# Hybrid decoder step, the last two output tiles split into 384 tokens and 136 in place of 260 and 260

## The reference, cut to what matters

```python
mix = concat([pm * silu(gp), a * silu(ga)], axis=-1)        # (tokens, 2048)
x = x + einsum('btm,md->btd', mix, w_out)                   # w_out: 2048 x 2048
y = x * rsqrt(mean(x * x, axis=-1) + 1e-6) * final_norm_g   # over all 2048 of a token
```

## Time and profile before

| | |
|---|---|
| median of 3 runs | 871.41 us (871.34 to 871.78) |
| the profiled execution | 871.79 us |
| its span | 869.8 us |
| TensorE matmul busy | 847.5 us, 97% of the span |
| VectorE, ScalarE, GpSimd busy | 545.9, 396.7, 40.1 us |
| granted TensorE clock, mean | 0.991 of full speed |

### The profile page before, as it was taken

One profiled execution on the slowest core, in us unless ns is written; L12 is line 12 of the kernel. 1 busy time (PEld: TensorE's weight loads), 2 busy tenths in 40 slices (PEclk: granted clock), 3 DMA queues, 4 the chain that ended last, 5 costly groups with the idle time before them and its releaser, 6 DMA issues.

```text
span 869.8 us, 17334 instructions
## 1 busy us (share of the span) xinstructions
PE 847.5 (97%) x6974; PEld 840.3 (97%) x6974; DVE 545.9 (63%) x1107; ACT 396.7 (46%) x917; POOL 40.1 (5%) x72
## 2 busy tenths in 40 slices
PE   7999999999999999999999999999999999999993
PEld 7999999999999999999999999999999999999993
DVE  5645875696668568747966785778877343333333
ACT  5745436523543454355345424543563444434332
POOL 2000000000000000000000001000000000000001
PEclk9999999999999999999999999999999999999997
DMA  9574266337525643563385247526658434334425
GB/s 289 149 178 129 83 157 158 102 107 175 143 82 137 186 120 95 151 168 108 89 187 141 86 135 196 136 75 150 172 161 281 139 95 129 113 115 120 135 62 196
DMA packets 207303, 122.45 MB, mean 141 GB/s; under 512 B 6552, under 2 KB 200608, under 8 KB 207200
## 3 DMA queue, kind: packets, MB, share of 16 engines
q1 hardware_dynamic: 204152, 113.86, 48.2%
q0 software_dynamic: 3072, 7.49, 2.5%
HBM read 106.59 MB, written 15.20 MB: 140 GB/s over the span
## 4 chain that ended last, share of the span: by engine, by line
PE 95%; DVE 2%; issue 1%; ACT 1%; DMA 1%; SPq 0%; DVEq 0%; ACTq 0%
PE pj L582 79%; PE ps_t L611 3%; PE pj L605 3%; PE ps_m L611 2%; PE ps_o L654 1%; PE ps_s L626 1%; PE ps_s L624 1%; PE ps_o L652 1%; PE ps_s L671 1%; PE ps_s L582 1%; PE ps_t L671 1%; PE ps_o L582 1%; DMA arena<-in_x_prompt 1%; PE pj L546 1%; DVE arena L1302 0%
## 5 line engine op out<-in xcount | busy, mean ns | idle before, releaser
L582 PE MATMUL pj<-mov_hi,w_hi 128*128 128x260 f32 x1952 | 403.8, 288 | 0.0
L582 PE MATMUL pj<-mov_hi,w_lo 128*128 128x260 f32 x1952 | 393.2, 283 | 0.0
L582 PE MATMUL pj<-mov_lo,w_hi 128*128 128x260 f32 x1952 | 392.5, 283 | 0.0
L582 PEld LDWEIGHTS pj<-mov_hi,w_hi 128*128 128x128 f32 x1952 | 300.9, 189 | 0.9
L582 PEld LDWEIGHTS pj<-mov_lo,w_hi 128*128 128x128 f32 x1952 | 301.3, 189 | 0.0
L582 PEld LDWEIGHTS pj<-mov_hi,w_lo 128*128 128x128 f32 x1952 | 301.0, 189 | 0.0
L1196 DVE TENSOR_TENSOR w_lo<-w_raw,w_hi 128x768 fp32r<-128x768 f32 (+1 forms) x189 | 163.5, 865 | 162.4 <-ACT w_hi L801 160.9
L801 ACT ACTIVATE w_hi<-w_raw 128x768 fp32r<-128x768 f32 (+1 forms) x189 | 145.7, 771 | 213.0 <-PE pj L582 195.6
L857 ACT ACTIVATE pt_hi<-ps_t 128x128 fp32r<-128x128 f32 (+1 forms) x64 | 26.2, 436 | 79.6 <-PE ps_t L611 75.4
L1279 DVE TENSOR_TENSOR pt_lo<-ps_t,pt_hi 128x128 fp32r<-128x128 f32 (+1 forms) x64 | 29.6, 483 | 43.2 <-ACT pt_hi L857 43.2
L1228 DVE SCALAR_TENSOR_TENSOR arena<-pj,rstd_bc 128x260 f32<-128x260 f32 (+2 forms) x104 | 36.9, 398 | 19.4 <-PE pj L582 17.8
(11 more groups left out here) (213 smaller groups left out, 806.3 us busy)
## 6 DMA issues: line engine op xcount, KB each, us to landing
w_raw<-in_w_in SPq DMA_DIRECT2D x96, 320.0 KB, 3.6
w_raw<-in_w_in SPq DMA_DIRECT2D x48, 384.0 KB, 3.8
arena<-in_cache_k_win SPq DMA_DIRECT2D x16, 384.0 KB
arena<-in_cache_v_win SPq DMA_DIRECT2D x16, 384.0 KB
w_raw<-in_w_out SPq DMA_DIRECT2D x16, 384.0 KB, 3.4
w_raw<-in_w_out SPq DMA_DIRECT2D x16, 320.0 KB, 3.1
arena<-in_cache_k_win SPq DMA_DIRECT2D x8, 512.0 KB
arena<-in_cache_v_win SPq DMA_DIRECT2D x8, 512.0 KB
```

The lines of the kernel that those rows point to most:

```text
L582: mm = pe.matmul(dst[h][:, 0:HT], w, m[:, k, HT * h:HT * h + HT], start=(k == 0 and i == 0), stop=(c == 2 and k == KT - 1 and i == 2))
```

## The change

The boundary between the two parts moves from token column 260 to 384 (HALF). Part 0 has 384 columns, row groups 0, 1 and 2; part 1 has 136, row group 3 and the samples. All that was laid out by halves follows: the transposes, evictions, adds and GpSimd's multiplications are 3 row groups wide in part 0 and 1 in part 1. ScalarE squares row groups 0 and 2 in part 0 and only the samples in part 1, VectorE squares row group 1 and then 3. In part 0 VectorE scales both halves of row group 0 and the first of 2, ScalarE both of 1 and the second of 2; in part 1 VectorE scales the first half of row group 3 (and the samples), ScalarE the second. Six stores of 512 KB follow part 0, two and the samples' follow part 1. The number of matmuls, their weights and the order on TensorE are the same.

```diff
+HALF = (0, 3 * P, NT)
@@ SP
-            for h in range(2):
-                for i, part in enumerate((slice(0, D_HALF), slice(D_HALF, D_MODEL))):
-                    sp.wait_ge(f_out, 2 * h + i + 1)
-                    sp.dma_start(yp[:, 2 * h, part], y[:, 2 * h, part]).then_inc(f_st, 16)
-                    sp.wait_ge(f_out_a, 2 * h + i + 1)
-                    sp.dma_start(yp[:, 2 * h + 1, part], y[:, 2 * h + 1, part]).then_inc(f_st, 16)
+            first, second = slice(0, D_HALF), slice(D_HALF, D_MODEL)
+            for i, (t, part, u, other) in enumerate(((0, first, 1, first), (0, second, 1, second),
+                                                     (2, first, 2, second), (3, first, 3, second))):
+                sp.wait_ge(f_out, i + 1)
+                sp.dma_start(yp[:, t, part], y[:, t, part]).then_inc(f_st, 16)
+                sp.wait_ge(f_out_a, i + 1)
+                sp.dma_start(yp[:, u, other], y[:, u, other]).then_inc(f_st, 16)
@@ TensorE, half_chunk and turn_half
-                        mm = pe.matmul(out_bank(d)[h][:, 0:HT], w, m[:, k, HT * h:HT * h + HT],
+                        mm = pe.matmul(out_bank(d)[h][:, 0:HALF[h + 1] - HALF[h]], w,
+                                       m[:, k, HALF[h]:HALF[h + 1]],
-                for t in (0, 1) if h == 0 else (2, 3):
+                for t in (0, 1, 2) if h == 0 else (3,):
@@ ScalarE, half_evict, half_squares and the scaling
-                act.activation(y_t[q][:, HT * h:HT * h + HT], out_bank(d)[h][:, 0:HT],
+                act.activation(y_t[q][:, HALF[h]:HALF[h + 1]], out_bank(d)[h][:, 0:HALF[h + 1] - HALF[h]],
-                for i, t in enumerate((0,) if h == 0 else (2, QT)):
+                for i, t in enumerate((0, 2) if h == 0 else (QT,)):
-                        act.wait_ge(half_sq, h + i)
+                        act.wait_ge(half_sq, 2 * h + i)
-                own = slice(2, 5) if h else slice(0, 2)
+                own = slice(3, 5) if h else slice(0, 3)
-                t = 2 * h + 1
-                for part in (slice(0, D_HALF), slice(D_HALF, D_MODEL)):
+                first, second = slice(0, D_HALF), slice(D_HALF, D_MODEL)
+                for t, part in ((1, first), (1, second), (2, second)) if h == 0 else ((3, second),):
@@ GpSimd
-                own = slice(2 * h, 2 * h + 2)
-                pool.wait_ge(half_sq, 1 + 2 * h)
+                own = slice(3 * h, 3 + h)
+                pool.wait_ge(half_sq, 2 + h)
-                    o = pool.tensor_tensor(ys, ys, gf.unsqueeze(1).to_broadcast([P, 2, P]), ALU.mult)
+                    o = pool.tensor_tensor(ys, ys, gf.unsqueeze(1).to_broadcast([P, 3 - 2 * h, P]), ALU.mult)
@@ VectorE, half_add (own and the widths alike), half_square and the scaling
-                own = slice(2 * h, 2 * h + 2)
+                own = slice(3 * h, 3 + h)
+                n = 3 - 2 * h
-                src = y[:, 2 * h + 1, P * (KT - 2):D_MODEL]
+                src = y[:, 1 + 2 * h, P * (KT - 2):D_MODEL]
-                dve.wait_ge(half_sq, 1 + 2 * h)
+                dve.wait_ge(half_sq, 2 + h)
-                for part in (slice(0, D_HALF), slice(D_HALF, D_MODEL)):
-                    dve.tensor_scalar(y[:, 2 * h, part], y[:, 2 * h, part],
-                                      rstd[:, 2 * h:2 * h + 1], None, ALU.mult).then_inc(f_out, 1)
+                for t, part in ((0, first), (0, second), (2, first)) if h == 0 else ((3, first),):
+                    dve.tensor_scalar(y[:, t, part], y[:, t, part], rstd[:, t:t + 1], None,
+                                      ALU.mult).then_inc(f_out, 1)
```

More of the change, by code:

```diff
@@ L1655, in half_add @@
                     y[:, own, cols],
-                    rows_from[:, 2 * P * h:2 * P * h + 2 * P].rearrange("p (t x) -> p t x", t=2),
-                    x_res[d % 3][:, 2 * P * h:2 * P * h + 2 * P].rearrange("p (t x) -> p t x", t=2),
+                    rows_from[:, 3 * P * h:3 * P + P * h].rearrange("p (t x) -> p t x", t=n),
+                    x_res[d % 3][:, 3 * P * h:3 * P + P * h].rearrange("p (t x) -> p t x", t=n),
                     ALU.add)
```

## The result

The changed kernel takes 877.80 us (median of 6, 876.88 to 878.25), the kernel before beside it 871.61 (871.34 to 872.24): ratio 1.0070, interval 1.0059 to 1.0081. It is slower by 6.2 us. The profiled execution took 876.88, the fastest of the six, with a span of 875.1; against the profiled one of before that is 5.1 us, and this is what the trace can explain. The other runs are 0.9 to 1.4 us longer still, at a mean granted clock of 0.988 against 0.991; where they lose it, no trace shows.

The account below looks back on a forecast made before the run. It took TensorE as the bound, 95% of the path that ended last. Last matmul 6.9 us later, chain 1.25 and stores 2.6 shorter make 3.1; the clock's 1.8 makes 4.9 on 871.41: 876.3 us, range 873.4 to 878.0.

Parts of the forecast that it names:

- The step of a matmul: TensorE, last two tiles: 0.176 us per matmul of 384 columns, 0.11 per matmul of 136, from 0.119 at 260.
- Rival C: TensorE, second part: weight load hides under 136 columns, 0.062 us each; not slower, 872.2 us; chance 0.10.
- Back-to-back issue gap: Skill's rule for a warm matmul, N/2.4 + 2.5 ns; by it the new split would be free on TensorE.
- The new wait: TensorE, second part: waits 2.1 us before tile 14's transposes for ScalarE's eviction, queued behind three scalings.
- The clock: Behind the new wait: granted clock falls to the 1.2 GHz level for 3.3 us, adding 1.8 us; bounds 0 and 3.5.
- Rival B: Last matmuls: the wait without the clock's fall, 874.5 us, own range 873.4 to 875.6; chance 0.30.
- The chain behind the last matmul: From the last matmul to the row scaling: shorter by 1.25 us, 4.47 in place of 5.72.
- The stores: From the scaling to the span's end: 2.6 us shorter, 6.2 in place of 8.78; the six early stores hide.
- Rival D: End of kernel: early stores still queued when the last ones come; up to 2 us more; chance 0.04.
- The sum: Whole kernel's end: 3.1 us later plus 1.8 for the clock, 4.9 us in all, giving 876.3.
- the split without its wait: Last two tiles: 3.1 us less the wait of 2.1, by the reflection's sum +1.0 us.

Follow-up runs that it names:

- e2: e1 with the second part's matmuls 232 columns wide in place of 136, the first 96 columns of the result thrown away: 872.01 us.
- e1: The changed kernel with ScalarE evicting the second part's tile 14 right after the first part's square root, ahead of its three scalings: 872.11 us, ratio to before 1.0002.
- e3c: The changed kernel, wait kept, with the second part's matmuls 232 columns wide; the same kernel as e3b, timed: 875.85 us (4 runs), ratio to before 1.0048.
- e3b: The changed kernel, wait kept, with the second part's matmuls 232 columns wide in place of 136; a single run: 874.67 us.
- e4: e1 with token ranges turned round: row groups 1 to 3 and the samples first (392 columns), row group 0 second (128): 873.75 us, ratio to before 1.0025.
- e6: e4 with tokens as loaded operand and weights moving in the second part, so no eviction or transposes there: 873.45 us, ratio to before 1.0017.
- e7: e6 with both tiles' weights moving as 256 columns for 10 of 16 blocks, GpSimd scaling the samples: 877.25 us, ratio to before 1.0063.
- e8: e4 with GpSimd's gain multiplications waiting for VectorE's mean: 873.63 us, ratio to before 1.0021.

## Why the prediction was right

It said 876.3 with 873.4 to 878.0, slower with 0.86; the median is 877.8, near the upper end. Point by point, from the second part's start T (848.16 in the trace after):

- **The step of a matmul.** Forecast 0.176 and 0.11; measured 0.176 (96 of them and eight transposes in 17.69 us, forecast 17.94) and 0.112. Right, and e2 shows that the columns don't set it; the loads' spacing says that the load does. Rival C is out: it needed less than 0.082. The Trainium skill has, in "TensorE: Matmul & The Clock Gate", section "LDWEIGHTS", P/1.2 ns for a load of P columns, by that estimate 107 ns for 128; the 0.112 here at 2.4 GHz is near it, the 0.213 at 1.2 GHz is not. The rule from "Back-to-back issue gap" that the prediction set against the rows does not agree. That section gives it for a matmul by itself, and some 81 ns for a stream of loads and matmuls at 128 columns, which is also below the 0.112.
- **The new wait.** Forecast 2.1 us before tile 14's transposes, from T + 7.65 to T + 9.76; measured from T + 7.62 to T + 10.16, 2.37 of it idle by the bracket. Right in place and cause (e1). The 0.4 at the far end is the scaling's start, T + 6.71 and not 6.29: GpSimd's multiplies of 384 columns are 0.98 and not 0.83, the mean 0.84, and one step of the root 0.47, where the same step took 0.22 before.
- **The clock.** Forecast: it falls, for about 3.3 us, +1.8. It fell and stayed; the work behind the wait took 6.25 us (858.32 to 864.57) where I had 3.56 + 1.65. This is the term that was mis-sized, by 1.0 us; my bound for it had 3.5 as the upper end. e3c shows the fall as I had priced it, among wider matmuls. The row I took it from was one of matmuls of 260 columns, and I carried it over to 136 without a row that showed it. It was also one of two outcomes: behind that same wait the clock fell in eight traces of thirteen. For the longer new wait the count is two of three. That the forecast time took in the fall was thus in part luck. Rival B (no fall) is possible as well: e3b, with wide matmuls, shows it once.
- **The chain behind the last matmul.** Forecast 4.47; measured 4.32 (864.57 to 868.89), at the lower clock.
- **The stores.** Forecast 6.2 from the scaling to the end, measured 6.21; the early ones did hide. Rival D did not come true here, but in e4, e6, e7 and e8.
- **The sum.** The trace gives 5.3 us on the span (4.9 forecast): the first part 5.4 longer, the second with its wait and its slow clock 4.4, the chain 1.4 shorter and the stores 2.6, and the first part starts 0.5 earlier than before. No step of mine had this last term. It comes from the clock: it did not fall behind the wait at 631.91, which left 0.5 us by 657.13 (657.61 before), though TensorE then waited 1.38 us for VectorE, 0.56 before. So the clock's term was 1.0 too small at the end, and a fall that stayed away earlier hid half of it. In the other five runs the mean clock of 0.988 is what a further fall of 3.4 us would give, by my estimate from the stretches in the trace; with it the 0.5 would be gone, and some 0.4 of the 0.9 by which the median exceeds the profiled run stay unexplained. No trace shows it.

What I had too pessimistic is the split without its wait: +1.0 by my sum (3.1 less the wait of 2.1), while e1 is at 1.0002 with an interval to 1.0011, which just reaches it.

## What to carry to other kernels

A matmul with a load of its own has a floor (0.11 us here for 128, 136 and 232 columns), and narrowing below it gives nothing back: moving columns from a piece above the floor to one below it costs the full price on one side (5.4 us here) and returns 0.8 on the other. When a stage in front grows, look at what stands behind it in each engine's queue: here the 0.14 us of slack of one eviction behind a row of scalings turned into 2.4 us of wait and, through the clock, 2.9 more, and moving that one instruction gave all of it back. And count the stores from the first one: once they run without a gap, a faster end of the computation is worth nothing.

## What the runs showed of the hardware that I had not expected

- The same wait of 1.76 to 1.78 us was followed by a fall of the granted clock to 0.50 in four traces and not in five, and one of 2.34 to 2.37 in two of three. Where it fell, it was down for 3.4 us each of the eight times behind the first wait and among matmuls of 232 columns (e3c), and for 5.6 us, until the work ended, among those of 136, although these step every 0.21 us at that level as those of 232 do. The step of either is that of a load of 128 columns, 0.112 at 2.4 GHz and 0.213 at 1.2 GHz, so the load goes with the clock.
- A VectorE instruction on four numbers can last 2.5 us beside GpSimd's stream: 2.61 (e4, the mean), 2.50 (e8, a step of the root), each until the last of four GpSimd instructions in a row had ended. Three scalings of 1024 columns took 5.51 us beside one of GpSimd's of 3.59, and 2.08 alone.
- Issues on SP's queue get longer as stores pile up: 0.35, 0.43, 0.79, then 1.19 us each for 512 KB, near the 1.29 that 512 KB take at 406 GB/s.
